# Gate columns behind half blocks, half-array products side by side, and the norm weights of stage B applied by column, in a three-layer decoder kernel in float32

## The reference

```python
def mlstm_mixer(u, w_in, b_gates, g_out, w_out):        # layer 0, stage A
    q, k, v, o, gl = jnp.split(u @ w_in, [...], axis=-1)  # 512 + 512 + 1024 + 1024 + 8 columns
    gl = gl.astype(F32) + b_gates                         # the last 8 columns are gates
    ...                                                   # chunked gated memory

def moba_mixer(u, positions, w_in, g_q, g_k, w_out):    # layer 1, stage B
    q, k, v = jnp.split(u @ w_in, 3, axis=-1)             # 8 heads of 128
    qh = rotary(rmsnorm(split_heads(q, h), g_q), positions, ROPE_DIMS, ROPE_THETA)  # 32 of 128 turned
    kh = rotary(rmsnorm(split_heads(k, h), g_k), positions, ROPE_DIMS, ROPE_THETA)
    p = jax.nn.softmax(s_own, axis=-1); out = p @ v       # causal, one block

# layer 2, stage C: three branches of one projection h @ w_in
def window_attention(q, k, v, sink):    # 8 query heads of 64, 2 key heads, window, sink
    p = jax.nn.softmax(jnp.concatenate([s, sink_b], axis=-1), axis=-1)[..., :-1]
    return jnp.einsum('bnhgqk,bnkhd->bnqhgd', p, vb)
def hyena_filters(L, w1, b1, f1, w2, b2, f2, w3):       # needs no x, computed during stage A
    h = jnp.sin(f1 * (z @ w1 + b1))
    h = jnp.sin(f2 * (h @ w2 + b2))
    h = (h @ w3).reshape(L, HY_ORDER, HY_DIRS, HY_WIDTH)  # two directions of 512, of two orders
    c = concatenate([fwd[:1] + bwd[:1], fwd[1:], 0, bwd[1:][::-1]])
def diff_attention(q, k, v, lam): ...
```

## Time and profile before

| | us |
|---|---|
| median of the runs (lowest, highest) | 1089.72 (1089.44, 1089.85) |
| profiled execution, its own time | 1089.0 |
| its span, first to last instruction | 1087.1 |
| mean granted clock of TensorE | 0.995 |
| PE busy, share of the span | 1069.8, 98% |
| DVE busy, share | 726.7, 67% |
| ACT busy, share | 539.7, 50% |
| POOL busy, share | 37.1, 3% |

### The profile page before, as it was taken

One profiled execution on the slowest core, in us unless ns is written; L12 is line 12 of the kernel. 1 busy time (PEld: TensorE's weight loads), 2 busy tenths in 40 slices (PEclk: granted clock), 3 DMA queues, 4 the chain that ended last, 5 costly groups with the idle time before them and its releaser, 6 DMA issues.

```text
span 1087.1 us, 14671 instructions
## 1 busy us (share of the span) xinstructions
PE 1069.8 (98%) x4952; PEld 865.4 (80%) x4952; DVE 726.7 (67%) x1224; ACT 539.7 (50%) x829; POOL 37.1 (3%) x40
## 2 busy tenths in 40 slices
PE   8899999999999999999999999999999999999998
PEld 7677678888888778788888888887777888888886
DVE  5756875455557997754555578988868877454553
ACT  6454554444445546644444465547457546444452
POOL 3112000000000210000000000000000000000000
PEclk9899999999999999999999999999999999999999
DMA  9454255565665544455655553544444365655653
GB/s 287 120 167 148 79 167 182 192 190 178 191 193 172 163 152 133 153 180 192 190 178 191 194 172 114 160 155 136 136 138 152 129 199 177 191 182 188 192 184 107
DMA packets 133599, 182.18 MB, mean 168 GB/s; under 512 B 11446, under 2 KB 80322, under 8 KB 133490
## 3 DMA queue, kind: packets, MB, share of 16 engines
q1 hardware_dynamic: 132090, 178.32, 51.7%
q0 software_dynamic: 1056, 2.70, 1.2%
q10 hardware_dynamic: 408, 0.56, 0.1%
HBM read 180.49 MB, written 1.05 MB: 167 GB/s over the span
## 4 chain that ended last, share of the span: by engine, by line
PE 89%; DVE 7%; ACT 2%; issue 1%; DMA 1%; POOL 0%; SPq 0%; DVEq 0%; POOLq 0%; ACTq 0%
PE ps L1844 17%; PE ps L1855 16%; PE ps L1847 16%; PE ps L1865 7%; PE ps L1866 7%; PE ps L1870 7%; PE ps L1829 2%; PE ps L1831 2%; PE ps L1830 2%; DVE wlo L1013 2%; PE ps L1939 1%; PE ps L1922 1%; ACT whi L538 1%; PE ps L2402 1%; PE ps L2069 1%
## 5 line engine op out<-in xcount | busy, mean ns | idle before, releaser
L1013 DVE TENSOR_TENSOR wlo<-raw,whi 128x1024 fp32r<-128x1024 f32 (+1 forms) x338 | 403.7, 1225 | 106.3 <-ACT whi L538 105.3
L538 ACT ACTIVATE whi<-raw 128x1024 fp32r<-128x1024 f32 (+1 forms) x338 | 342.2, 1053 | 102.6 <-DMA raw<-in_ffn_w_out 28.2
L1844 PE MATMUL ps<-whi,ath 128*128 128x512 f32 (+1 forms) x896 | 357.9, 400 | 3.1 <-ACT whi L538 1.4
L1847 PE MATMUL ps<-whi,atl 128*128 128x512 f32 (+1 forms) x896 | 349.7, 391 | 0.0
L1855 PE MATMUL ps<-wlo,ath 128*128 128x512 f32 (+1 forms) x896 | 240.6, 390 | 0.0
L1844 PEld LDWEIGHTS ps<-whi,ath 128*128 128x128 f32 x896 | 168.9, 189 | 47.1 <-issue 8.3
L1855 PEld LDWEIGHTS ps<-wlo,ath 128*128 128x128 f32 x896 | 167.7, 188 | 35.4 <-DVE wlo L1013 0.5
L1847 PEld LDWEIGHTS ps<-whi,atl 128*128 128x128 f32 x896 | 169.1, 189 | 33.0 <-issue 0.5
L1865 PE MATMUL ps<-whi,brh 128*128 128x512 f32 x272 | 106.5, 392 | 0.4 <-issue 0.4
L1866 PE MATMUL ps<-whi,brl 128*128 128x512 f32 x272 | 105.9, 389 | 0.0
L1089 DVE TENSOR_TENSOR brl<-ps,brh 128x512 fp32r<-128x512 f32 x33 | 22.8, 692 | 93.7 <-ACT brh L584 93.7
(11 more groups left out here) (344 smaller groups left out, 1009.1 us busy)
## 6 DMA issues: line engine op xcount, KB each, us to landing
raw<-in_ffn_w_in SPq DMA_DIRECT2D x176, 256.0 KB, 2.9
raw<-in_ffn_w SPq DMA_DIRECT2D x132, 256.0 KB, 2.9
raw<-in_w_in SPq DMA_DIRECT2D x104, 256.0 KB, 2.9
raw<-in_ffn_w_out SPq DMA_DIRECT2D x88, 256.0 KB, 2.8
raw<-in_a_w_in SPq DMA_DIRECT2D x48, 256.0 KB, 4.1
raw<-in_b_w_in SPq DMA_DIRECT2D x48, 256.0 KB, 3.0
raw<-in_a_w_out SPq DMA_DIRECT2D x16, 256.0 KB, 2.9
raw<-in_b_w_out SPq DMA_DIRECT2D x16, 256.0 KB, 2.8
```

The source lines that it names most:

```text
L538: a_(unit_view(whi, slot, w), unit_view(raw, slot, w), ACT.Copy).then_inc(hi_ready, 1)
L1013: v_.tensor_tensor(unit_view(wlo, slot, w), unit_view(raw, slot, w), unit_view(whi, slot, w), ALU.subtract).then_inc(lo_ready, 1)
L1844: mm(ps[bk + t][:, 0:w], ath[:, k, t * P:(t + 1) * P], rh[:, kk, :], start=k == 0, stop=False)
L1847: mm(ps[bk + t][:, 0:w], atl[:, k, t * P:(t + 1) * P], rh[:, kk, :], start=False, stop=False)
```

## The change

1. The gate columns come with the units. A slot of the ring has 16 floats more. Units 4 to 7 are loaded by three DMAs, the third with 8 columns for each half, and split with the rest (1040 columns). `gate_units` replaces `units(1)`: each product of 512 columns becomes one of 256 and one of 264, whose last 8 are the gates. Left halves go to banks 2 and 3, right halves with gates to 6 and 7. `wg`, its load and its split go.
2. `filt_w3` is loaded twice, into partitions 0 to 63 and 64 to 127, and one DVE instruction over 128 partitions forms sum and difference. The second filter layer has its weights twice side by side, so that the hidden layer lies on both halves, and `filter3` takes sum and difference from different halves of the array. POOL's two instructions go. The decay table is loaded later.
3. In stage B the norm weights of the 96 unrotated columns are applied by a scale for each partition in `b_copy`, after the turn. DVE multiplies only the 32 rotated columns by `B_T1` (128x128). POOL's eight instructions go. The reductions (`b_sums`) stand behind the additions, the tables ahead of the splits of two units, and the last unit of block 10 behind `b_turn(2)` and `b_turn(3)`. Exp is called once early, and `b_down` of head 0 waits for the fourth copy only ahead of its last bank.
4. The window attention handles scores and `w_pv` for a pair of heads at once, products of the two halves in turn. The logits have four buffers instead of two, and the order on ACT and DVE is written out anew.
5. ACT splits units 8 and 9 ahead of the first sine, DVE unit 8 ahead of `filter_arg(0)`; PE waits for `glog` behind the turn of the queries.

The two multiplying passes over 64 partitions are gone, and the loads wait for units 8 and 10. The diff, cut to its core:

```diff
             def load_in(u0, w, n0, nw=512):
...
+                    if u0 + i in GATE_UNITS:
+                        nc.sync.dma_start(v[:, :, 512:], w.rearrange("(k p) n -> p k n", p=P)[:, 2 * i:2 * i + 2, 3072:])\
+                            .then_inc(raw_loaded[(u0 + i) % RING], 16)
...
-            for d, op in enumerate((ALU.add, ALU.subtract)):
-                nc.gpsimd.tensor_tensor(A_ws[:, :, d, :], A_w3[:, :, 0, :], A_w3[:, :, 1, :], op).then_inc(sem("w3_ready"), 1)
...
-                    nc.gpsimd.tensor_tensor(y, y, B_T1[:, kind, t, :].unsqueeze(1).to_broadcast([P, 4, BD]),
-                                            ALU.mult).then_inc(sem("b_scaled"), 1)
...
             feed(5 + AHEAD)
             evac(0, lambda t: A_qk[:, t, 0:512])
...
-            feed(7 + AHEAD)
+            feed(9 + AHEAD)
             act.wait_ge(sem("f_arg"), 1)
...
+            v_.scalar_tensor_tensor(A_ws, A_w3[:, :, 1, :], sign, A_w3[:, :, 0, :], ALU.mult, ALU.add)\
+                .then_inc(sem("w3_ready"), 1)
...
+            def gate_units(lo, hi):
+                for c in range(lo, hi):
...
+                    for kk, t in ((0, 0), (1, 0), (0, 1), (1, 1)):
+                        k = 2 * c + kk
+                        for act, first in ((ath, k == 0), (atl, False)):
+                            a = act[:, k, t * P:(t + 1) * P]
+                            mm(ps[2 + t][:, 0:256], a, rh[:, kk, 0:256], start=first, stop=False)
+                            mm(ps[6 + t][:, 0:256 + GATES], a, rh[:, kk, 256:], start=first, stop=False)
...
+            gate_units(0, 2)
...
-            pe.wait_ge(sem("glog"), 2)
-            turn_qk(0, 0)
-
-            pe.wait_ge(sem("f_arg"), 1)
+            pe.wait_ge(sem("f_arg"), 1)
+            turn_qk(0, 0)
+            pe.wait_ge(sem("glog"), 2)
+            pe.wait_ge(sem("right_copied"), 1)
...
                 for d in range(2):
-                    ins = mm(ps[(4, 6)[q] + d][:, :], fil[:, 3, :].rearrange("p (j q) -> p q j", q=2)[:, q, :],
-                             A_ws[:, o, d, :], start=True, stop=True)
+                    rows = slice(64 * d, 64 * d + 64)
+                    ins = mm(ps[(4, 6)[q] + d][:, :], fil[rows, 3, :].rearrange("p (j q) -> p q j", q=2)[:, q, :],
+                             A_ws[rows, o, :], start=True, stop=True)
...
-            units(10)
+            units(10, 0, 3)
             b_turn(2)
             b_turn(3)
+            units(10, 3, 4)
...
+            def w_scores(i):
...
                 for t in range(NT):
-                    ins = mm(ps[4 + h % 2][:, t * S:(t + 1) * S], C_qT[rows, pr, t * P:(t + 1) * P], C_kT[rows, g, :],
-                             start=True, stop=True)
+                    for f in range(2):
+                        rows = slice(64 * f, 64 * f + 64)
+                        ins = mm(ps[4 + f][:, t * S:(t + 1) * S], C_qT[rows, i, t * P:(t + 1) * P],
+                                 C_kT[rows, i // 2, :], start=True, stop=True)
...
                 for s in range(2):
+                    for f in range(2):
+                        rows = slice(64 * f, 64 * f + 64)
+                        ins = mm(ps[2 + i % 2][rows, 0:S], C_pa[:, s, 640 + g * HD:640 + (g + 1) * HD],
+                                 C_PT[:, f, s * S:(s + 1) * S], start=(s == 0), stop=(s == 1))
...
+            for i, block in enumerate((20, 21, 22)):
+                units(block, 2, 4)
+                w_turn(2 * i + 2)
+                if i < 2:
+                    w_scores(i + 2)
+                w_pv(i)
+                if i < 2:
+                    units(block + 1, 0, 2)
+                    w_turn(2 * i + 3)
```

More of the change, by code:

```diff
@@ L345, in build, with loaded @@
         sil_ready, hid_ready = sem("sil_ready"), sem("hid_ready")
+        GATE_UNITS = range(U_A + 4, U_A + 8)
         def unit_view(tile, slot, w):
-            return tile[:, slot, :].rearrange("p (k n) -> p k n", k=2)[:, :, 0:w]
+            n = max(w, 512)
+            return tile[:, slot, 0:2 * n].rearrange("p (k n) -> p k n", k=2)[:, :, 0:w]
+        def loaded(u):
+            return 32 * (u // RING + 1) + (16 if any(g <= u and (u - g) % RING == 0 for g in GATE_UNITS) else 0)
         def unit_width(u):
-            return 256 if U_C + 12 <= u < U_C + 16 else 512
+            return 256 if U_C + 12 <= u < U_C + 16 else 512 + GATES if u in GATE_UNITS else 512
         block = ctx.enter_context(nc.Block())
@@ L763, in _ @@
             feed(U_B + 21)
+            a_(sm[:, 126:127], con[:, 0:1], ACT.Exp)
             b_copy(2)
@@ L1370, in b_rotate @@
                     rsqrt(sm[:, 416 + 16 * kind:432 + 16 * kind], 16)
-                for t in range(NT):
-                    y = dst[:, t, half * 512:(half + 1) * 512].rearrange("p (h d) -> p h d", h=4)
-                    dve.wait_ge(sem("b_scaled"), 2 * b + t + 1)
-                    v_.tensor_tensor(y[:, :, 0:BROT], y[:, :, 0:BROT], B_z[:, t, :, :], ALU.add)\
-                        .then_inc(sem("b_rotated"), 1)
             def b_knorm(half):
@@ new lines, in _ @@
+            w_logits(0)
+            feed(U_C + 32)
+            w_prob(0)
+            w_logits(1)
+            feed(W_STEPS[0])
+            w_prob(1)
+            w_logits(2)
+            feed(W_STEPS[1])
+            w_logits(3)
+            dve.wait_ge(sem("h_hi"), 1)
+            v_.tensor_tensor(obl[:, :, :], h_v, obh[:, :, :], ALU.subtract).then_inc(sem("h_lo"), 1)
+            w_prob(2)
+            feed(W_STEPS[2])
+            c_sums(3, C_z, 320, 16)
+            w_prob(3)
+            w_logits(4)
@@ new lines, in _ @@
+            feed(W_STEPS[3])
+            w_out(0)
+            w_logits(5)
+            c_sums(4, hid_flat, 336, 8)
+            c_sums(5, sil_flat, 344, 8)
+            w_prob(4)
+            feed(W_STEPS[4])
+            dve.wait_ge(sem("c_ssq"), 6)
+            link(v_.tensor_scalar(rq_a[:, 0:32], sm[:, 320:352], 1.0 / HD, EPS, ALU.mult, ALU.add))
+            rsqrt(sm[:, 320:352], 32)
+            w_prob(5)
+            w_logits(6)
+            feed(W_STEPS[5])
+            w_out(1)
+            w_logits(7)
@@ L1852, in up_unit, with down_unit @@
                     k = 2 * i + kk
-                    if beside is not None:
-                        beside(k, t, 2)
                     ins = mm(ps[bk + t][:, 0:w], ath[:, k, t * P:(t + 1) * P], rl[:, kk, :], start=False, stop=k == KT - 1)
                 ins.then_inc(unit_used, 1)
-            def down_unit(slot, k, first, last, ready, act_h, act_l, banks=DOWN_BANKS):
+            def down_unit(slot, k, first, last, ready, act_h, act_l, banks=DOWN_BANKS, last_bank=None):
                 pe.wait_ge(hi_ready, ready)
@@ L1863, in down_unit @@
                     for t in range(NT):
+                        if last_bank is not None and (nb, t) == (1, NT - 1):
+                            last_bank()
                         o = ps[banks[2 * nb + t]][:, :]
```

357 lines of the change are left out of this document (173 added, 184 removed).

## The result

The changed kernel took 1078.47 us (median of 4 runs, 1077.25 to 1079.42); the kernel before 1089.58 in the same comparison. The ratio is 0.9909, 95% interval 0.9889 to 0.9929. The direction was right, but 1078.47 lies above the predicted range of 1060.5 to 1071.0. The profiled execution took 1077.25 us, its span 1075.4 against 1087.1. Of all the executions in this document one is left out, of `b_act768`, which took 1785.9 us at a mean granted clock of 0.555, where its seven others took 1083.8 to 1089.4 us.

What follows compares the result with a forecast made beforehand. PE, busy for 98% of the span, was taken to bound the kernel. Six savings, 5.0 + 3.8 + 3.9 + 3.4 + 3.1 + 6.8 = 26.0 us off 1089.0, gave 1063.0, median 1063.7 us; range 1060.5 to 1071.0.

Steps and rivals of the forecast that it cites:

- gate units: Block 1: products of 256 and 264 columns replace the 12 small gate products per unit; 5.0 us saved in four units.
- wait of stage A: PE's 4.05 us wait for glog ahead of the turn of the queries shrinks to 0.3; 3.8 us saved.
- clock behind it: Stage A, 42.47 to 51.16 us: without the 4 us gap the granted clock doesn't fall; 3.9 us saved.
- filter3: Second filter layer's sum and difference run side by side in different array halves; 0.86 us saved each, 3.4 in four.
- stage B: PE's waits of 1.5 us for DVE's addition and 1.3 for the copies go; 3.1 us saved net.
- window attention: Paired heads: fewer score slots save 3.2 us and paired w_pv 3.6; together 6.8 us.
- the wait moves and stays: Rival, stage A: units 8 to 11, needed 9 us earlier, come late; 4 to 8 us, 1068 to 1072; 12%.
- the first rival: Rival, window attention: the column halves of w_pv don't run side by side; costs 3.6 us, 1067.3; 10%.
- DVE in the window attention: Rival: DVE, 59.15 of 60.4 us busy, is late and PE waits; 3 to 6.8 us, 1066.7 to 1070.5; 17%.
- slower than before: Rival, window attention: PE waits for DVE at head turns and the clock falls, 6 us or more a head; 1094; 2%.

Runs made afterwards that it cites:

- b_act768: Kernel before with 192 unused floats behind whi, so that x and the activations begin 768 bytes later; ratio 0.9974 to the kernel before.
- a_by_head: Changed kernel with slots of 1088 floats, and in paired scores and w_pv all products of one array half ahead of the other's; 1067.16 us.
- a_pad128: Changed kernel, slots still 1040 floats, with 32 unused floats between raw and whi so whi's slots match wlo's modulo 256 bytes; 1080.01 us.
- after_again: The changed kernel measured once more, unedited, as a control on one chip with other kernels; 1078.57 us.

## Why the prediction was wrong, point by point

**The step that failed** is in the part on the gates: "DVE and ACT split 16 columns more in four units ...: nothing". I priced the 16 floats of a slot as work for two engines, and not as what they do to the place of all tensors behind. No term and no rival held a slower product of 512 columns. It cost 13.6 us between the profiled spans (1075.4 against 1061.8 with slots of 1152), though in stage A PE waited 0.4 less in the changed kernel. By the distances, 3.9 ns on some 3,820, it would be 15; about 1 us of this I can't place.

The other terms, from the profiles:

| term | predicted | measured | from |
|---|---|---|---|
| gate units | 5.0 | 5.2 | 38.42 - 20.90 before, 33.24 - 20.88 after |
| wait of stage A | 3.8 | 1.9 | 4.05 before, 2.15 after |
| clock behind it | 3.9 | 3.5 | queries to keys 11.42 before, 10.09 - 2.15 after |
| `filter3` | 3.4 | 3.4 | 1.99 and 1.14, four times |
| stage B | 3.1 | 3.7 | lead from 14.1 to 17.8, slots of 1152 |
| window attention | 6.8 | 7.6 | lead from 17.8 to 25.4, slots of 1152 |

**Stage A's wait.** The chain over `filter_arg` was read rightly: without POOL's pass `glog` is off it. (That pass made sums and differences; the section on the change calls it multiplying.) What I took as 0.3 us, the chain of copies, has a load in it. The rival "the wait moves and stays" named the cause, loads and splits of units 8 to 11 needed 9 us earlier; of its price only the wait came in the changed kernel, and the clock's part in the profiles of `a_by_head` and `a_pad128`. The prediction called itself wrong if a wait over 2 us stood in 20 to 60 us, with a clock below 1.0 behind it: the wait was there, 2.15 us, and the clock stayed at 1.00 (both windows, 30 to 40 and 40 to 50).

**The clock's 3.9 us** are the price in one execution. The profiled kernel before had 0.52 in 40 to 50 us; `b_act768`, the same program but for places, stood 4.15 us at the same wait and had 0.83:

```profile
40.00:50.00 10.00, 7.40 (x31) 5.50 (x32) 8.54 (x18) 5.35 (x7) 0.00 (x0) 0.83 0.14 48
```

Its span was 1084.7 us and not 1087.1. So the execution against which the sum was made was one of the dear ones, and against one like that of `b_act768` this term is worth less than 3.5.

**Side by side.** The two heads of `w_pv` do run in different column halves at once, into one bank, eight passes in 1.08 us:

```profile
745.55 1.08 PE L2452 MATMUL ps<-work 128*64 128x256 f32 x8
```

So the first rival falls. The Trainium skill (page TensorEngine Tiling (Array Packing), section Gotcha 1: PSUM Pressure) says that different row tiles can't reach the same bank at once; carried over to column tiles, as that rival had it, this does not hold here.

Of the 7.6 us the fewer slots of scores gave 3.3 (7.6 us in all before, 4.2 with slots of 1152) and those of `w_pv` 3.8 (7.8 and 4.0). Another 0.7 came from a place that the sum had left out, the turns:

```profile
737.97 0.60 PE L2437 MATMUL ps<-con,work 128*128 128x128 f32 x4
738.33 0.47 PE L1877 MATMUL ps<-whi,ath 128*128 128x512 f32 x1
...
743.95 0.60 PE L2437 MATMUL ps<-con,work 128*128 128x128 f32 x4
744.49 1.13 PE L2427 MATMUL ps<-work 64*128 64x256 f32 x8
```

Four passes of a turn cost 0.36 us if a unit follows and 0.53 if scores or `w_pv` follow; before, all eight turns cost 0.53, now four. So a change of form costs about 0.2 us, and the fewer there are, the more is gained: 7.6 us instead of the 6.0 of array time alone. The Trainium skill (same page, section Tiling Modes) says that a change of the tiling mode drains the engine; the trace agrees with it in kind.

**DVE in the window attention.** With slots of 1152 PE needed 59.5 us from the first scores on to the turns behind the last `w_pv`, where I had worked out 60.4; DVE had 57.11 in it, without PE waiting:

```profile
714.90:774.40 59.50, 59.50 (x301) 46.20 (x301) 57.11 (x119) 42.26 (x85) 0.00 (x0) 1.00 0.47 151
```

**Stage B.** Both waits of the earlier trace rows are gone and none took their place.

**The rival "slower than before"** did not occur: no wait over 1 us in stages B and C.

The forecast of 1063.7 us is 1.3 to 1.5 from what the change takes once its slots are 1088 or 1152 floats long. That is no credit for the prediction: what was asked was this change, with 1040. It is in part luck, too. Against the profiled execution the gain is 25.3 us by the spans (1087.1 and 1061.8), near the 26.0 of the sum, but against the medians of the kernel before in the same comparisons (1087.70 and 1086.29) it is 22.7 and 21.1.

One bound was worked out wrongly: 96 products dearer by 0.02 us are 1.9 us, so the lower bound of the gates is 3.2 and not 3.5. Nothing hangs on it.

## What to carry to other kernels

A change in the size of one tensor is a change in the address of all that are allocated behind it; where products of fp32r with 512 columns bound the kernel, as here, keep what PE streams and what it loads as weights at the same place modulo 256 bytes, every slot of a ring too, and pad the slot if need be. Other types were not measured. When a kernel gains in some places and its lead melts steadily in between, count instructions in equal windows of an untouched loop, since busy shares can't show a slower pace. And behind an instruction that can stand at a load, put nothing that the bounding engine is about to need.

## What the runs showed of the hardware that I had not expected

- Products of 128 x 128 by 512 columns of fp32r start 226 or 227 ns apart if the operands agree modulo 256 bytes, and 231 to 233 on average if not; a distance of 64 bytes costs more (233.3) than one of 128 (232.4). At 256 columns the effect doesn't show.
- PE runs the products of two halves of the array at once, into one bank too if they are column halves, even where all of one half stand ahead of the other's in its program, at least over four passes.
- The granted clock stayed at 1.00 behind PE's waits of 1.78, 2.15, 2.5 and, in `after_again`, 2.85 us in stage A, and fell behind those of 2.66 (`a_pad128`, 0.92 and 0.91 in the two windows), 2.76 and 4.05. So the length of the wait alone does not tell whether the clock falls.
